# A hybrid attention encoder layer: five projection steps ahead of the first scores, q ahead of v, and a first weight tile in three transfers

## What is computed

```
u = rmsnorm(x, g_pre_mix)
proj = u @ w_in                      # columns: qa ka va qb kb vb qc kc vc
ya = diff_attention(qa, ka, va)      # 4 heads, two softmaxes each, p0 - lam * p1, causal by chunks
yb = sliding_window_sink_attention(qb, kb, vb)   # 8 heads, 2 kv heads, band of 2 chunks, sinks
yc = chunk_band_attention(qc, kc, vc)            # 8 heads, band of 9 chunks
gates = sigmoid(u @ w_gate + b_gate)
mixed = gates0 * (ya @ w_proj_a) + gates1 * (yb @ w_proj_b) + gates2 * (yc @ w_proj_c)
h = x + rmsnorm(mixed @ w_out, g_post_mix)
u = rmsnorm(h, g_pre_ffn)
gate, up = split(conv3(u @ w_ffn_up) + conv_b)
out = h + rmsnorm((gelu(gate) * up) @ w_ffn_down, g_post_ffn)
```

## Time and profile before

| | us |
|---|---|
| median of 3 executions | 847.74 (846.5 to 848.87) |
| the profiled execution | 847.32 |
| its span, first to last instruction | 845.5 |
| PE busy in the span | 833.3 |
| DVE, ACT, POOL busy | 651.2, 478.9, 399.9 |
| mean granted clock of PE | 0.996 of full speed |

### The profile page before, as it was taken

How to read it: one execution, slowest core, us unless ns; L and a number is a source line. 1 busy time by engine, 2 the same in 40 slices (tenths; PEclk the granted TensorE clock), 3 DMA queues, 4 the chain that set the end, 5 groups by cost and what they waited for, 6 DMA issues and landing times.

```text
span 845.5 us, 13419 instructions
## 1 busy us (share of the span) xinstructions
PE 833.3 (99%) x4701; PEld 728.2 (86%) x4701; DVE 651.2 (77%) x1261; ACT 478.9 (57%) x904; POOL 399.9 (47%) x511
## 2 busy tenths in 40 slices
PE   8899999999999999999999999999999999999997
PEld 7788888888888888999998889899999999988885
DVE  6567777888876777975544279988888888999995
ACT  5456656777766754544444446455565656555662
POOL 6454434424443437887667434766565656010002
PEclk9999999999999999999999999999999999999999
DMA  7621233232223213333334741555553434396584
GB/s 232 178 75 53 73 99 99 74 99 81 68 74 79 64 52 98 89 113 113 116 109 166 224 158 49 170 168 171 167 175 114 131 110 137 130 325 216 176 290 153
DMA packets 138055, 111.35 MB, mean 132 GB/s; under 512 B 7591, under 2 KB 121199, under 8 KB 136708
## 3 DMA queue, kind: packets, MB, share of 16 engines
q1 hardware_dynamic: 136362, 102.05, 39.5%
q0 software_dynamic: 720, 5.24, 1.7%
q10 hardware_dynamic: 906, 3.20, 1.0%
HBM read 97.05 MB, written 13.42 MB: 131 GB/s over the span
## 4 chain that ended last, share of the span: by engine, by line
PE 96%; DVE 2%; DMA 1%; ACT 1%; POOL 0%; issue 0%; SPq 0%; DVEq 0%
PE banks L2299 24%; PE banks L2301 24%; PE banks L2300 24%; PE banks L2598 3%; PE banks L2599 3%; PE banks L2600 3%; PE banks L2474 2%; PE banks L2382 2%; PE banks L2383 2%; PE banks L2769 1%; PE banks L2768 1%; PE banks L2767 1%; PE banks L2446 1%; PE banks L2484 1%; PE banks L2453 1%; DMA ring_raw<-in_w_in_dram 1%
## 5 line engine op out<-in xcount | busy, mean ns | idle before, releaser
L862 POOL TENSOR_TENSOR ring_lo<-ring_raw,ring_hi 128x256 fp32r<-128x256 f32 x380 | 311.2, 851 | 283.4 <-ACT ring_hi L1018 283.1
L2299 PE MATMUL banks<-u_hi,ring_hi 128*128 128x512 f32 (+1 forms) x580 | 222.7, 384 | 0.0
L2301 PE MATMUL banks<-u_hi,ring_lo 128*128 128x512 f32 (+1 forms) x580 | 217.9, 376 | 0.0
L2300 PE MATMUL banks<-u_lo,ring_hi 128*128 128x512 f32 (+1 forms) x580 | 217.6, 375 | 0.0
L2301 PEld LDWEIGHTS banks<-u_hi,ring_lo 128*128 128x128 f32 x580 | 109.4, 189 | 20.2
L2300 PEld LDWEIGHTS banks<-u_lo,ring_hi 128*128 128x128 f32 x580 | 109.9, 189 | 18.1
L2299 PEld LDWEIGHTS banks<-u_hi,ring_hi 128*128 128x128 f32 x580 | 109.7, 189 | 17.9
L1018 ACT CAST ring_hi<-ring_raw 128x1024 fp32r<-128x1024 f32 x96 | 100.2, 1044 | 40.0 <-PE banks L2301 23.6
L2120 DVE SCALAR_TENSOR_TENSOR wide<-banks,cols,wide 128x511 f32<-128x511 f32 x88 | 64.6, 744 | 3.5 <-ACT wide L1381 1.6
L2299 PE MATMUL banks<-pages,ring_hi 128*128 128x512 f32 (+1 forms) x180 | 61.2, 340 | 0.0
L2300 PE MATMUL banks<-pages,ring_hi 128*128 128x512 f32 (+1 forms) x180 | 61.2, 340 | 0.0
(11 more groups left out here) (334 smaller groups left out, 2021.0 us busy)
## 6 DMA issues: line engine op xcount, KB each, us to landing
ring_raw<-in_w_ffn_up_dram SPq DMA_DIRECT2D x88, 256.0 KB, 3.5
ring_raw<-in_w_in_dram SPq DMA_DIRECT2D x60, 256.0 KB, 3.4
ring_raw<-in_w_ffn_down_dram SPq DMA_DIRECT2D x55, 256.0 KB, 3.7
ring_raw<-in_w_gate_dram SPq DMA_DIRECT2D x48, 256.0 KB, 3.3
split_tokens<-pages SPq DMA_DIRECT2D x5, 1024.0 KB, 6.8
pages<-split_tokens POOLq DMA_DIRECT2D x5, 1024.0 KB, 5.8
ring_raw<-in_w_out_dram SPq DMA_DIRECT2D x16, 256.0 KB, 3.1
second_tokens<-wide SPq DMA_DIRECT2D x10, 384.0 KB, 4.0
```

Of the source, the lines that this page charges most:

```text
L862: last = pool.tensor_tensor(wlo[:, r, c], raw[:, r, c], whi[:, r, c].bitcast(F32), ALU.subtract)
L2299: pe.matmul(out, lhs_hi, rhs_hi, start=start, stop=False)
L2300: pe.matmul(out, lhs_hi, rhs_lo, start=False, stop=False)
L2301: return pe.matmul(out, lhs_lo, rhs_hi, start=False, stop=stop)
```

## The change

- The projection steps ahead of the first scores grow from 32 to 37 (`STEPS_AHEAD = 5`): the first five of the eight steps of q1. All later steps move up by five places in the slots of units 0 to 7, whose cuts are unchanged; the slots of units 8 to 10 get 20 steps each instead of 23, 22 and 22, those of unit 11 get 16 instead of 14.
- In the order of tiles, q of a unit comes ahead of its v, for units 2 to 8 (before: v, q, k, and v, k, q for unit 8). With the shift, q of the next unit but one ends in a unit's last slot, v of the next unit in its first and k in its third; k of unit 1 ends in slot 1 instead of 2, and q of unit 1 in slot 0 instead of 1.
- The first weight tile comes in three transfers: one of 256 KB with a semaphore of its own (`first_raw`), two of 128 KB. ACT rounds its first half as soon as the first transfer has landed, then the first half of the turned tokens, then the second half of the weights. POOL's low quarters and PE's first value products wait for the halves separately.
- The small tables' semaphores are regrouped: five loads count on one, and PE waits once for all of them; the order of the loads is the same.

```diff
-GEMM_ORDER = ("va0 vb0 q0 k0 q1 k1 v2 q2 k2 v3 q3 k3 v4 q4 k4 v5 q5 k5 v6 q6 k6 v7 q7 k7 v8 k8 q8 "
+GEMM_ORDER = ("va0 vb0 q0 k0 q1 k1 q2 v2 k2 q3 v3 k3 q4 v4 k4 q5 v5 k5 q6 v6 k6 q7 v7 k7 q8 v8 k8 "
               "gate0 q9 gate1 gate2 q10 gate3 gate4 q11 gate5 gate6 gate7")
 SLOT_CUTS = ((0, 5, 11, 17, 23),) + 3 * ((0, 5, 11, 17, 24),) + 4 * ((0, 5, 10, 17, 24),) + (
-    (0, 6, 11, 17, 23), (0, 5, 11, 16, 22), (0, 5, 11, 16, 22), (0, 3, 7, 10, 14))
+    (0, 5, 10, 15, 20), (0, 5, 10, 15, 20), (0, 5, 10, 15, 20), (0, 4, 8, 12, 16))
+STEPS_AHEAD = 5
...
-    steps, at = {-1: flat[:RING * KT]}, RING * KT
+    at = RING * KT + STEPS_AHEAD
+    steps = {-1: flat[:at]}
...
             def by_k_wide(t, r, src):
-                load(t, r, (dst[:, 0:2, :], dst[:, 2:4, :]), (src[:, 0:2, :], src[:, 2:4, :]))
+                if t == 0:
+                    sp.dma_start(dst[:, 0:2, :], src[:, 0:2, :]).then_inc(first_raw, 16)
+                    load(t, r, (dst[:, 2, :], dst[:, 3, :]), (src[:, 2, :], src[:, 3, :]))
+                else:
+                    load(t, r, (dst[:, 0:2, :], dst[:, 2:4, :]), (src[:, 0:2, :], src[:, 2:4, :]))
...
-            w_lo(0, 0)
+            pool.wait_ge(first_half_hi, 1)
+            w_lo_quarter(0, 0)
+            w_lo_quarter(0, 1)
+            pool.wait_ge(w_hi_done, 1)
+            w_lo_quarter(0, 2)
+            w_lo_quarter(0, 3).then_inc(w_lo_done, 1)
...
-            w_hi_at(0)
+            act.wait_ge(first_raw, 16)
+            act.copy(whi[:, 0, 0:512], raw[:, 0, 0:512]).then_inc(first_half_hi, 1)
             act.wait_ge(first_turned, 1)
             act.copy(u_hi[:, 0:4, 0:P], turned_tokens(0, 0)[:, 0:4, :]).then_inc(u_first_hi, 1)
+            act.wait_ge(raw_loaded[0], 32)
+            act.copy(whi[:, 0, 512:1024], raw[:, 0, 512:1024]).then_inc(w_hi_done, 1)
...
-                for i, loads in ((0, 1), (1, 1), (3, 3)):
-                    pe.wait_ge(small_loaded[i], 16 * loads)
+                pe.wait_ge(small_loaded[3], 5 * 16)
...
+            pe.wait_ge(first_half_hi, 1)
             pe.wait_ge(u_first_hi, 1)
+            value_products(0, u_hi, whi, range(2))
             pe.wait_ge(w_hi_done, 1)
-            value_products(0, u_hi, whi, first)
+            value_products(0, u_hi, whi, range(2, 4))
             turn_tokens(1, 0, x_tok[:, 1, :])
```

More of the change, by code:

```diff
@@ L459, in build_encoder @@
         x_loaded = [sem(f"x_loaded{t}") for t in range(TT)]
-        small_loaded = [sem(f"small_loaded{i}") for i in range(7)]
+        small_loaded = [sem(f"small_loaded{i}") for i in range(5)]
         raw_loaded = [sem(f"raw_loaded{r}") for r in range(RING)]
@@ L469, in build_encoder @@
         w_lo_done = sem("w_lo_done")
+        first_raw = sem("first_raw")
+        first_half_hi = sem("first_half_hi")
         xs_first = sem("xs_first")
@@ L636, in load_small @@
             def load_small():
-                sp.dma_start(t5_in, t5_table).then_inc(small_loaded[0], 16)
-                sp.dma_start(crel_in, c_rel_table[0].rearrange("(a p) h -> p a h", p=64)).then_inc(small_loaded[1], 16)
+                sp.dma_start(t5_in, t5_table).then_inc(small_loaded[3], 16)
+                sp.dma_start(crel_in, c_rel_table[0].rearrange("(a p) h -> p a h", p=64)).then_inc(small_loaded[3], 16)
                 sp.dma_start(conv_in[:, 0:3, :], conv_w[0].rearrange("c (j n) -> j c n", n=P)).then_inc(small_loaded[3], 16)
@@ L643, in load_small @@
                     sp.dma_start(lam_in[:, i, :], v[0].partition_broadcast(P)).then_inc(small_loaded[4], 16)
-                sp.dma_start(sink[:], sinks[0].partition_broadcast(P)).then_inc(small_loaded[6], 16)
-                sp.dma_start(sub_raw[:], subln_g[0].rearrange("(n a) -> n a", a=1)).then_inc(small_loaded[5], 16)
+                sp.dma_start(sink[:], sinks[0].partition_broadcast(P)).then_inc(small_loaded[1], 16)
+                sp.dma_start(sub_raw[:], subln_g[0].rearrange("(n a) -> n a", a=1)).then_inc(small_loaded[0], 16)
             def load(t, r, dst, src):
@@ L1629, in tables @@
                 dve.tensor_scalar(neg_lam[:], lam_dif[:], -LAM_INIT, None, ALU.add).then_inc(lam_done, 1)
-                dve.wait_ge(small_loaded[5], 16)
+                dve.wait_ge(small_loaded[0], 16)
                 dve.tensor_scalar(sub_col[:], sub_raw[:], 1.0 - LAM_INIT, None, ALU.mult).then_inc(lam_done, 1)
-                dve.wait_ge(small_loaded[6], 16)
+                dve.wait_ge(small_loaded[1], 16)
                 dve.tensor_scalar(neg_sink[:], sink[:], -1.0, None, ALU.mult).then_inc(lam_done, 1)
```

## The result

The change makes the kernel slower. The median after is 853.61 us (853.44 to 854.08, four executions) against 847.12 us before (846.15 to 848.87, four): a ratio of 1.0075 with the interval [1.0057, 1.0094], 6.5 us lost. The prediction was 842.3 us, with 5.4 won. The profiled execution took 853.44 us, its span is 851.6.

A forecast was written before the change was run, and what follows sets the result against it. PE was taken as the bound, busy 833.3 of 845.5 us. 2.94 + 1.68 + 0.96 + 0.2 - 0.4 = 5.4 us off 847.32 gives 841.9; the median lies 0.4 higher, so 842.3, range 840.5 to 844.5.

The forecast's parts named there:

- The filler: Between k0 and the first scores: 15 matmuls of q1 fill PE's wait, gaining 2.94 us.
- The clock: Behind the first scores: without a standstill PE's clock stays full instead of at half rate, gaining 1.68 us.
- The start: First weight tile in halves: PE starts earlier, low products of token tile 1 at about 14.00, gaining 0.96 us.
- the loss of 1 us: At the start: 2 us of fixed cost added once in front of token tile 2; not taken into the sum.
- q1 in slot 0: q1's casts, 2.42 us, stand on ACT ahead of slot 1's `probs_high`; some 0.2 us of room left, nothing charged.
- the last units: Units 8 to 11: with four steps in a slot, the 0.2 us wait of slot 46 goes.
- q ahead of v: Units' last slots: q's casts and subtractions move there, work unchanged; 0.4 us charged, at worst 9.7.
- the wait charged with 0.4: PE at `pv` behind slots 19, 23 and 27: about 0.1 to 0.2 us each, 0.4 in all.
- the room for `probs_low`: Behind slot 23: `probs_low` ends at 183.68, PE wants it at `pv` at 185.06, 1.38 us of room.
- DVE becomes the bound in the last slots: Rival: PE waits at `pv` of each unit's first slot, 1.38 us in seven units, 851.6 us; chance 0.06.
- The last sentence of the prediction: Refuting sign: a PE wait over 1 us behind the first scores, or the clock falling again ahead of the end.

The follow-up runs named there:

- turns in the gap: Kernel before with 24 transposes of the identity on PE between k0 and the first scores; 846.22 us against 847.7, ratio 0.9986.
- the start alone: Kernel before with only the three transfers, rounding by halves and regrouped semaphores; 846.18 us against 846.75, ratio 0.9991.
- two steps ahead: Changed kernel with STEPS_AHEAD 2 instead of 5, the last unit's slots getting the other three steps; 847.82 us against 846.75, ratio 1.0012.
- k's low part at once: Changed kernel with DVE making the low part of k in the slot where its tile ends; 842.41 us against 846.75, ratio 0.9945.
- no steps ahead: Changed kernel with STEPS_AHEAD 0 and the slot cuts of before, new order and three transfers kept; 849.48 us against 846.75, ratio 1.003.

## Why the prediction was wrong

Right, with what it measured:
- The filler: 15 matmuls end, and the first scores follow at 39.39 without a wait. Predicted 39.9.
- The clock: 1.00 from 37 to 45 us, and a mean of 0.998 over the span instead of 0.996. The turns in the gap show that the standstill was the cause.
- The start, in its places: first value product 8.98 (8.7 predicted), low products of token tile 1 at 13.50 (14.0). Its gain of 0.96 is not shown: over nine profiles it is about 0.7, and the start alone measured 0.9991 [0.998, 1.0003]. The Trainium skill's fit of about 2 us of fixed cost to each transfer (DMA: Bandwidth & Descriptors, "Anatomy of one DMA") is for transfers issued through GpSimd; those here are issued by SyncE, and the loss of 1 us that the prediction estimated from the fit is not in these medians.
- q1 in slot 0, and the last units: no wait in unit 0 and none behind slot 45.

Wrong is the step "q ahead of v", in what it left out and in one reading. It says that the work of ACT and DVE "stays the same, its slot changes", and costs only that: which casts and subtractions are queued ahead of which. It doesn't ask what else hangs on the place of a tile's last step. A tile's bank comes free when its low part is made, and the tile two places on wants it. I had the row for the right question: the low part of a k is made in the slot behind the one in which it ended, which the description of the kernel says. And I used the bank as a condition for the filler (q1's bank) but for no later tile. Moving all steps by five moves the demand for the bank into the last slot, and leaves its release where it was. The cost is seven times 1.5 to 1.9 us, 11.8 in all; 5.4 - 11.8 gives 6.4 slower, and 6.5 were measured. That it comes so near is partly luck: the 0.96 of the start in the 5.4 is not shown, and the wait charged with 0.4 is not in the trace of after.

The reading that was wrong is the room for `probs_low`. The prediction lets it end at 183.68 and takes `pv`, at 185.06, for the first that wants it. The timeline of PE before has the turn of v ahead of that:

```profile
183.92 0.60 PE L2394 MATMUL banks<-ident,v_feat 128*128 128x128 f32 x4
```

The room was 183.92 - 183.68 = 0.24 us and not 1.38. With the prediction's own 1.44 us in front the wait would be 1.2 us behind each of three slots, 3.6 in all instead of 0.4. With two steps ahead 4.0 were lost so, at four slots; with k's low part at once, which takes work out of the last slot, 0.9.

The rival "DVE becomes the bound in the last slots" had the number of places right (seven), the sign, and a price near the true one (9.7 against 11.8); it got 6 in 100. Its place, `pv` of the following slot, is not where it happened: there the trace of after has no wait. So that its price lies near is luck. With two steps ahead its mechanism shows, at 4.0 us. It was judged by DVE's time in a slot; what decided was the place at which DVE gives the bank back, for with k's low part at once DVE does the same work, and 0.9 us of waits are left of it instead of 11.8. The last sentence of the prediction named what would refute it, waits of over 1 us behind the first scores, and seven of them are there.

The sum of the rest fits what k's low part at once measured: 4.3 us won, 0.0055 of the time with an interval from 0.0038 to 0.0071, where 5.4 us would be 0.0064. The profiles show losses that the sum does not have: 0.5 more than charged behind `probs_low`, and 1.4 by pitch in the feed-forward part, which the prediction hadn't looked at.

The Trainium skill has a sentence that fits such a trace (Perfetto Trace Analysis, "Optimization Strategy"): the same gap, repeated over a stretch on the engine that should be saturated, can mean that there is not enough SBUF or PSUM for the next tile. The trace agrees: seven gaps of 1.5 to 1.9 us, at the same step of seven units, all for a PSUM bank. Yet two banks are enough when one is given back a slot earlier, as k's low part at once shows.

## What to carry to other kernels

When a stream of tiles is shifted against the loop that serves it, list for each tile not only who makes its inputs and who needs its output, but also who wants its buffer next, and where in the loop the buffer is given back. With two buffers taking turns, the step that matters is the first of the tile two places on. When you read how much room a result has, look for the first instruction that waits for it, which need not be the one that uses it most. And a filler taken from later slots has a price in these slots: look at the engine that was nearly the bound there, and at the later stage that will end last once this one is shorter.

## What the runs showed of the hardware

PE's clock fell to 0.50 behind a standstill of 2.78 us (three kernels: before, the start alone, no steps ahead; 3.4 us at 1.2 GHz each time). It did not fall behind 1.43 us (two steps ahead), nor behind any of the seven waits of 1.3 to 1.7 us of after, nor when 24 transposes of the identity filled the gap. In front of all of these PE had been at work without a long break. Each of these is one profiled execution. The three with the fall have a mean granted clock of 0.996 or 0.997, the others 0.998 or 0.999; of the 25 executions of before that stand beside the start alone, 8 have 0.998 or more. So the fall may not come in every execution of before, and the gain of the filler would then be smaller in these; no trace of them was kept that would show it.
